# First unit of a two-block model kernel: one weight load in four pieces, four tiles computed together row by row

## The reference

```
hn  = x * rsqrt(mean(x*x) + 1e-6) * mix_norm
u   = hn @ lru_w_in + lru_b_in               # 1024 -> 2048: a gate branch and rec
rec = causal_depthwise_conv(rec, conv_w, conv_b)      # 4 taps
gl  = per-block product of rec with gate_w            # 4 blocks of 256
```

## Time and profile before

| | before |
|---|---|
| median of 3 runs | 1274.97 us (1273.9 to 1275.98) |
| profiled execution, its own time | 1278.19 us |
| span of its profile | 1276.4 us |
| PE busy | 1118.7 us (88%) |
| DVE busy | 684.6 us (54%) |
| ACT busy | 420.9 us (33%) |
| DMA, mean | 284 GB/s |

### The profile page before, as it was taken

One profiled execution on the slowest core, in us unless ns is written; L12 is line 12 of the kernel. 1 busy time (PEld: TensorE's weight loads), 2 busy tenths in 40 slices (PEclk: granted clock), 3 DMA queues, 4 the chain that ended last, 5 costly groups with the idle time before them and its releaser, 6 DMA issues.

```text
span 1276.4 us, 23114 instructions
## 1 busy us (share of the span) xinstructions
PE 1118.7 (88%) x9331; PEld 903.8 (71%) x9333; DVE 684.6 (54%) x1069; ACT 420.9 (33%) x532; POOL 32.5 (3%) x71
## 2 busy tenths in 40 slices
PE   9999999999999999999999999768766677666676
PEld 8999999999968999999998899433322233222232
DVE  5799988887345756557866877622112112112114
ACT  3775333345384433335634663510000000000001
POOL 0000000000000000001000000000000000000000
PEclk9999999999999999999999999889888888888889
DMA  9678988864530795550553337799999999999996
GB/s 348 225 270 299 341 301 302 302 260 164 174 125 1 264 316 197 172 171 2 208 196 132 133 141 263 288 385 416 428 427 428 428 430 427 430 428 428 428 427 253
DMA packets 99401, 362.48 MB, mean 284 GB/s; under 512 B 4160, under 2 KB 51664, under 8 KB 84112
## 3 DMA queue, kind: packets, MB, share of 16 engines
q1 hardware_dynamic: 95216, 335.06, 67.7%
q0 software_dynamic: 3984, 26.50, 5.3%
q10 hardware_dynamic: 144, 0.10, 0.0%
HBM read 360.58 MB, written 1.06 MB: 283 GB/s over the span
## 4 chain that ended last, share of the span: by engine, by line
PE 60%; DMA 24%; DVE 10%; ACT 3%; issue 2%; SPq 0%; POOLq 0%; DVEq 0%; POOL 0%; ACTq 0%
DMA wbuf<-in_w_up 22%; PE ps L1895 16%; PE ps L1818 9%; PE ps L1781 8%; PE ps L2229 7%; PE ps L2105 4%; DVE parts L1105 3%; PE ps L1802 3%; PE ps L1827 2%; PE ps L2249 2%; PE ps L2279 1%; PE ps L1771 1%; PE ps L2012 1%; DMA wbuf<-in_lru_w_in 1%; PE ps L1978 1%
## 5 line engine op out<-in xcount | busy, mean ns | idle before, releaser
L2229 PE MATMUL ps<-wbuf,big 128*32 128x256 f32 x2176 | 167.4, 473 | 108.4 <-DMA wbuf<-in_w_up 96.9
L1895 PE MATMUL ps<-big_parts,parts 128*128 128x256 f32 x2112 | 255.0, 282 | 1.2 <-DVE parts L1105 1.2
L1105 DVE TENSOR_TENSOR parts<-wbuf,parts 128x2048 fp32r<-128x2048 f32 x92 | 208.7, 2286 | 85.2 <-ACT parts L833 43.9
L1895 PEld LDWEIGHTS ps<-big_parts,parts 128*128 128x128 f32 x2112 | 252.4, 188 | 2.0 <-DVE parts L1105 1.2
L2229 PEld LDWEIGHTS ps<-wbuf,big 128*32 128x32 f32 x2176 | 85.7, 135 | 203.6 <-issue 103.0
L1691 DVE TENSOR_TENSOR big<-big,ps 128x128 f32<-128x128 f32 x33 | 9.5, 287 | 265.2 <-ACT big L1037 265.2
L1037 ACT ACTIVATE big<-ps 128x128 f32<-128x128 f32 x33 | 9.2, 277 | 417.2 <-PE ps L2229 417.2
L1818 PE MATMUL ps<-big_parts,parts 128*128 128x256 f32 x1088 | 132.9, 282 | 0.6 <-DVE parts L1105 0.6
L1818 PEld LDWEIGHTS ps<-big_parts,parts 128*128 128x128 f32 x1088 | 130.7, 188 | 0.8 <-DVE parts L1105 0.8
L1781 PE MATMUL ps<-parts_f,parts 128*128 128x256 f32 x704 | 98.3, 283 | 0.0
L1781 PEld LDWEIGHTS ps<-parts_f,parts 128*128 128x128 f32 x704 | 90.5, 192 | 0.2
(11 more groups left out here) (353 smaller groups left out, 1407.5 us busy)
## 6 DMA issues: line engine op xcount, KB each, us to landing
wbuf<-in_w_down SPq DMA_DIRECT2D x32, 2048.0 KB, 38.0
wbuf<-in_w_gate SPq DMA_DIRECT2D x31, 2048.0 KB, 32.7
wbuf<-in_w_up SPq DMA_DIRECT2D x31, 2048.0 KB, 37.2
wbuf<-in_ffn_w_in SPq DMA_DIRECT2D x44, 1024.0 KB, 12.0
wbuf<-in_w_ada POOLq DMA_DIRECT2D x24, 1024.0 KB, 8.8
wbuf<-in_ffn_w_out SPq DMA_DIRECT2D x22, 1024.0 KB, 4.9
wbuf<-in_w_in SPq DMA_DIRECT2D x10, 2048.0 KB, 7.9
wbuf<-in_attn_w_qkv SPq DMA_DIRECT2D x6, 2048.0 KB, 8.5
```

Of the source, the lines that this page charges most:

```text
L1105: nc.vector.tensor_tensor(lo, whole, hi.bitcast(F32), ALU.subtract).then_inc(done, 1)
L1895: ins = mm(ps[:, b, d * 256:(d + 1) * 256], w[pw][:, k, d * P:(d + 1) * P], h_part_of[px][:, k], start=(k == 0 and d == 0 and i == 0), sto ...
L2229: ins = mm(at, rows, gu_place[s][:, :, k, r * P:(r + 1) * P], start=(k == 0), stop=(k == KC - 1))
```

## The change

Unit rec0 is loaded in four transfers of two rows (k) each, with a semaphore of its own for each. The four semaphores are those of the last expert's parts, renamed to `quarter_loaded`; the last expert therefore waits for 16 + 32 instead of 32. `load_count` leaves rec0 out of the counts of its place. On PE, `norm_sums(0)`, the wait for rec0 and the two calls of `product_pair` are replaced by `first_products`: for each row k it multiplies all four blocks, so that tiles rec0 and rec1 grow together in two banks; the square sums stand behind row 1. The programs of DVE, ACT and POOL are the same as before.

```diff
-        last_loaded = [sem(f"last_loaded{j}") for j in range(LAST_PARTS)]
+        quarter_loaded = [sem(f"quarter_loaded{j}") for j in range(LAST_PARTS)]
...
-            load_count[name] = (s, 1 + sum(1 for m in load_count if load_count[m][0] == s and m not in ("gates", "ada")))
+            load_count[name] = (s, 1 + sum(1 for m in load_count if load_count[m][0] == s and m not in ("rec0", "gates", "ada")))
...
-            for name in ("rec0", "rec1", "gates"):
+            for q in range(LAST_PARTS):
+                ks = slice(q * KC // LAST_PARTS, (q + 1) * KC // LAST_PARTS)
+                sp.dma_start(unit_view("rec0")[:, ks], unit_source("rec0")[:, ks]).then_inc(quarter_loaded[q], 16)
+            for name in ("rec1", "gates"):
                 load_unit(name)
...
-            norm_sums(0)
-
-            def wide(nm, u, h):
-                product_pair(f"{nm}{2 * u + h}", unit_view(f"{nm}{u}"), 2 * h, KC, hT, 0 if (nm, u, h) == ("rec", 0, 0) else None)
+
+            def first_products():
+                w = unit_view("rec0")
+                for k in range(KC):
+                    if k * LAST_PARTS % KC == 0:
+                        pe.wait_ge(quarter_loaded[k * LAST_PARTS // KC], 16)
+                    wait_rows(0, k)
+                    for m in range(4):
+                        ins = mm(bank(f"rec{m // 2}")[:, m % 2 * 256:(m % 2 + 1) * 256], w[:, k, m * P:(m + 1) * P], hT[:, k], start=(k == 0 and m % 2 == 0),
+                                 stop=(k == KC - 1), skip_group_check=True)
+                        if k == KC - 1 and m % 2 == 1:
+                            ins.then_inc(tile_done, 1)
+                    if k == 1:
+                        norm_sums(0)
...
-            wait_unit(pe, "rec0")
-            for h in range(2):
-                wide("rec", 0, h)
+            first_products()
             pe.wait_ge(fh_lo, 1)
             wait_parts("rec1")
...
-                        pe.wait_ge(last_loaded[k * LAST_PARTS // KC], 32)
+                        pe.wait_ge(quarter_loaded[k * LAST_PARTS // KC], 16 + 32)
```

More of the change, by code:

```diff
@@ L608, in _ @@
                 for m, w in enumerate(("w_gate_2", "w_up_2")):
-                    sp.dma_start(gu_place[s][:, m, ks], a[w][0, e].rearrange("(p k) f -> p k f", k=KC)[:, ks]).then_inc(last_loaded[j], 16)
+                    sp.dma_start(gu_place[s][:, m, ks], a[w][0, e].rearrange("(p k) f -> p k f", k=KC)[:, ks]).then_inc(quarter_loaded[j], 16)
             sp.wait_ge(down_done[0], e + 1 - EXPERT_SLOTS)
@@ L1761, in wait_rows @@
                 pe.wait_ge(h_ready, KC * i + k + 1)
[L1763 to L1773, removed]
             def product_pair_parts(name, w, m, kn, rhs):
```

## The result

The changed kernel takes 1278.60 us (median of 13 runs, 1277.57 to 1281.20), the kernel before 1275.76 us in the same series (13 runs, 1273.42 to 1280.00). The ratio is 1.0022, 95% interval 1.0012 to 1.0032: slower by 2.8 us (1.5 to 4.1), just past the 2.55 us that the prediction took as the limit of what can be told from no change.

A forecast was written before the change was run, and what follows sets the result against it. TensorE was taken as the main bound (60% of the span, DMA 24%). Delay +2.20 us (-0.26 included) and clock +1.0 gave +3.2 on the median 1274.97: 1278.2 us; range 1275.9 to 1280.4 us (+0.9 to +5.4).

The forecast's parts named there:

- The order on the vector engine: Before the second unit: half 1 queues behind rec0's late scaling, TensorE stops 2.24 us; tiles end +2.20 us later overall.
- The restart: At the second unit's products on TensorE: starting again after the stop costs 0.22 us.
- The earlier start (-0.26): First unit: quarter 0 lands at 7.4, products follow the sums without waiting, TensorE ends 0.26 us earlier.
- Square sums and queues at no cost: First and second units: sums 3.5 us later and three more transfer issues cost nothing; second unit perhaps 0.5 us late, covered.
- The delay goes through whole: After tile rec3: the whole +2.20 us reaches conv(1), the gates and second gates, and the end.
- rival (c): Expert stage: its weight stream swallows the 2.2 us, leaving 1274.7 us, not slower; chance 0.08.
- The clock: Second unit's products: a lower granted clock after the stop costs 0 to 2.0 us, taken as +1.0.

The follow-up runs named there:

- e1: Changed kernel with lower half 1 of the second unit moved ahead of rec0's scaling on the vector engine; 1.0009 against the kernel before.
- e3: Changed kernel, but tile rec0 finished over all eight rows before rec1 is begun, pieces and early start kept; 1.0010 against the kernel before.
- e2: Kernel before with one added wait: the vector engine's scaling of tile rec0 also waits for tile rec1; 1.0047 against the kernel before.
- e11: e1 with the four transfers of constants and small rows issued behind gb1 instead of ahead of it; 0.9990 against the kernel before.
- e12: Changed kernel unaltered, run for a fourth profile; no time of its own given.
- e10: Changed kernel unaltered, timed a second time beside the kernel before and profiled a third time; 1.0022 against the kernel before.
- e9: Kernel before, unaltered, run for a second profile; the scalar engine's wait for gb1 was 0.35 us, no run time given.
- e7: Kernel before with the four transfers of constants and small rows issued behind gb1 instead of ahead of it; 1.0003 against the kernel before.
- e5: Changed kernel with an extra 2.28 us vector-engine instruction between rec0's scaling and lower half 1 of the second unit; 1.0038 against the kernel before.
- e4: Changed kernel with nine unread filler products on TensorE between the first and second unit; 1.0017 against the kernel before.
- e6: e3 with the four transfers of constants and small rows issued behind gb1 instead of ahead of it; 0.9985 against the kernel before.
- e8: Changed kernel unaltered, run for a second profile; no time of its own given.

## Why the prediction was right

The forecast was +3.2 us and 1278.2; measured +2.8 and 1278.60, within the range. The mechanism is the one forecast; how close the number came is in part luck. At the second gates the four profiles of the changed kernel (46.91, 47.49, 46.77, 48.60) lie 2.94 us on average behind the two of the kernel before (44.48, 44.53); 0.37 of it is the clock, 2.57 the rest. The prediction had 1.0 and 2.20, so one term was too large and the other too small. And the absolute time is near because the forecast started from 1274.97, where thirteen runs gave 1275.76. Step by step:

- *The order on the vector engine.* Right, and with what follows the stop the whole of the cost within the noise. Forecast: scaling of rec0 at 24.48, half 1 at 25.15, TensorE on at 27.56 after 2.24 us, tiles done at 39.30. Measured: 24.68, 25.35, 27.78, 2.27, 39.54. e1 and e3 remove the stop, e2 makes it alone, and e11 with the stop removed is clear of the changed kernel in time.
- *The restart.* Forecast 0.22 us, measured 11.76 - 11.52 = 0.24.
- *The earlier start (-0.26).* This term was wrong in both its parts; the error is 0.2 us in the first profile. Quarter 0 was forecast for 7.4, 1.35 us behind the input. It ended a wait of TensorE at 7.98 (e3), 8.05 (e11), 8.08 (e1) and 8.18 (e12), 1.7 to 2.0 us after the scalar engine had taken up the input; in e10 it was there by 7.83. The other estimate, 7.6 by the 341 GB/s that the Trainium skill gives for 1 MB ("DMA: Bandwidth & Descriptors", *Measured (HBM→SBUF, 128 partitions, SWDGE, issued from GpSimd)*), was too early as well. And I took the warm-up's end, 7.6, as fixed. It is not: the 40 warm-up records took 7.08 us after and 6.63 before, and the first product of the changed kernel came at 8.07, 8.64, 7.83 and 8.18 in its four profiles. In the kernel before, a later end of the warm-up moves nothing, since the first product waits for the whole unit anyway: it came at 11.50 and, with a warm-up of 7.22 us, at 11.66 (e9). The change gave that cover away. Its first unit ended at 25.51 in the first profile instead of the forecast 25.32, and at 25.36 to 26.07 in the four, against 25.58 and 25.64 in the kernel before: nothing was won.
- *Square sums and queues at no cost.* Right: the root chain ended at 16.69, the vector engine's small steps stood at 16.79 to 17.58, half 0 at 19.33 with 3.06 us of waiting behind it. The second unit came 0.5 us later (17.39 for 16.91), as the estimate from the slower stretch had it.
- *The delay goes through whole.* Right at first (+2.43 at 46.91 and at 120.15). Later in the same two profiles it was 1.98 (430.65 for 428.67), while two executions of the kernel before differ by 0.3 there, so hardly anything was swallowed by then. But rival (c) is about the expert stage, which comes after. There one set of 64 products (the chain's, near 878) starts at 878.39, 874.15 and 876.59 in the kernel before and in e7, and at 879.69, 877.57, 879.07 and 881.78 in the changed kernel: 3 us later on average, over a scatter of 4. With the timed 2.8 us of whole executions that leaves rival (c) no room for more than a small part. Its price was also off by the -0.26, which the +2.20 already held: swallowed whole, it would have left 1274.97. The ends of the range, +0.9 and +5.4, follow only roughly from the terms: half of 2.2 is 1.1, and 4.2 with one microsecond more is 5.2.
- *The clock.* The term of the sum that was mis-sized. I took the middle of 0 and 2.04, +1.0. The runs show two outcomes and no middle: 0 in three profiles, 1.48 us in the fourth. Were four profiles enough for a share, that would be 0.4 on average, and with the 2.57 us above that is 2.94, where 2.8 was timed: the same within the interval. Behind stops of 3.14 and 4.48 us (e2, e5) the clock fell as well, in one profile each.

What I did not see, in the expectations of e1 and e3, was the next wait in line. I asked what is late if the stop is there, and should also have asked what would be late without it. A wait of 0.33 us for gb1 stood in the trace of before; with the pieces and without the stop it was 2.3 and 3.1 us, and why it grew is open.

## What to carry to other kernels

Before two tiles are made to finish together, look at what stands behind the first one's evacuation in the consumer's program order: if TensorE itself waits for one of those instructions, it waits longer than the earlier start can give. An engine that waits only 0.26 us for a transfer, because other work fills the time, could win no more than that by getting it in pieces, and lost its cover against what varies ahead of it. When a wait is removed, ask the trace which wait comes within a microsecond of it: here another one took part of the gain until the transfers ahead of it were moved too.

## What the runs showed of the hardware

**The clock behind the same stop differs from one execution to the next.** The same program with the same 2.27 us stop kept 2.4 GHz in three profiled executions; in one it fell to 1.2 GHz for most of a stretch behind it (0.57 on the stretch's average), and the second unit's products took 1.48 us more.

**The pace of products differs between builds.** In the kernel before, the changed kernel, e2 and e7, the loop of the first feed-forward runs 96 products in 11.39 us; in e1, e3, e4, e5, e6 and e11 in 11.52, with no wait. The granted clock is 1.00 in such a round of the kernel before and of e1. Chain of waits of e1, then of the kernel before:

```profile
131.41 11.52 PE ps L1894 x96
142.93 5.76 PE ps L1809 x48
```

```profile
140.74 5.70 PE ps L1818 x48
146.44 11.39 PE ps L1895 x96
157.83 5.70 PE ps L1818 x48
```

It is the build and not the chip: e6, e7 and e8 ran on one chip, and e6 alone had the slow pace. TensorE's program is the same in e1 and in the changed kernel, only two instructions of the vector engine are swapped. From the loop's start to the last of its eight rounds (products at 117.72 and 260.36 in the kernel before, at 119.65 and 263.89 in e1) it is 1.6 us, so the times of those six kernels carry as much that is not from the mechanism under test. In the second feed-forward all of them run at 11.39. What decides it was not tried.

**The same 2 MB transfer landed 7.9 to 12.5 us after its issue.** Unit gb1, issued near 37.1 in all kernels without the stop, was used at 46.8 to 46.9 in the kernel before and e7 (landed 9.7 us after its issue), at 48.8 and 49.6 in e1 and e3 (11.6 and 12.5), and was there by 46.3 in e6 and e11 (8.3). In the four profiles of the changed kernel, issued at 39.55 and later, it took 7.9 to 8.1. Why, one profile of most of them does not tell.
